# The inverses of a chunked recurrence: 32x32 blocks on four tiles of TensorE's array instead of 64x64 blocks on two

## The reference

```python
def rwkv7_scan(r, logw, k, v, kk, a, s0):
    def step(s, inp):
        r_t, lw_t, k_t, v_t, kk_t, a_t = inp
        sa = jnp.einsum('bhvk,bhk->bhv', s, -kk_t)
        s = (s * jnp.exp(lw_t)[:, :, None, :] + sa[..., None] * (kk_t * a_t)[:, :, None, :]
             + v_t[..., None] * k_t[:, :, None, :])
        return s, jnp.einsum('bhvk,bhk->bhv', s, r_t)
```

## Time and profile before

| | |
|---|---|
| median of 3 executions | 1626.25 us (1624.93 to 1627.86) |
| span of the profiled execution, first to last instruction | 1624.6 us |
| span plus what lies around it, at the median | 1626.25 us, so 1.65 us around |
| TensorE busy | 1540.8 us, 95% of the span |
| VectorE busy | 557.3 us, 34% |
| ScalarE busy | 298.2 us, 18% |

### The profile page before, as it was taken

One profiled execution on the slowest core, in us unless ns is written; L12 is line 12 of the kernel. 1 busy time (PEld: TensorE's weight loads), 2 busy tenths in 40 slices (PEclk: granted clock), 3 DMA queues, 4 the chain that ended last, 5 costly groups with the idle time before them and its releaser, 6 DMA issues.

```text
span 1624.6 us, 61645 instructions
## 1 busy us (share of the span) xinstructions
PE 1540.8 (95%) x27605; PEld 1373.6 (85%) x27605; DVE 557.3 (34%) x1410; ACT 298.2 (18%) x801; POOL 16.4 (1%) x32
## 2 busy tenths in 40 slices
PE   5999898999997999999988899999999999999995
PEld 3888476999546788988877898999999999999995
DVE  1463425666635354565771321010100101010102
ACT  2012422100111512434323201010101001010101
POOL 0000000000000000000000000000000000000000
PEclk9999999999999999999999899999999999999998
DMA  9722666444456233000123399999999999999993
GB/s 392 270 94 96 263 256 260 178 186 157 181 195 259 78 105 144 5 7 5 33 98 115 124 413 381 390 412 387 418 381 417 384 418 377 418 378 418 367 419 142
DMA packets 72892, 407.02 MB, mean 251 GB/s; under 512 B 10514, under 2 KB 10948, under 8 KB 35908
## 3 DMA queue, kind: packets, MB, share of 16 engines
q1 hardware_dynamic: 68176, 398.92, 62.0%
q0 software_dynamic: 1184, 3.41, 0.7%
q10 hardware_dynamic: 3412, 2.93, 0.5%
HBM read 403.31 MB, written 1.92 MB: 249 GB/s over the span
## 4 chain that ended last, share of the span: by engine, by line
PE 81%; PEld 10%; DVE 3%; ACT 2%; issue 2%; DMA 1%; ACTq 0%; PEldq 0%; DVEq 0%; POOL 0%
PE bank L1416 20%; PE bank L1436 10%; PE bank L953 8%; PEld bank L1416 6%; PE bank L986 4%; PE bank L625 4%; PE bank L628 4%; PEld bank L1436 3%; PE bank L730 3%; PE bank L733 3%; PE bank L1165 2%; PE bank L1125 2%; PE bank L651 2%; PE bank L755 2%; PE bank L1161 2%; PE bank L1150 2%
## 5 line engine op out<-in xcount | busy, mean ns | idle before, releaser
L1416 PE MATMUL bank<-w,ring 128*64 128x86 f32 x11264 | 455.0, 237 | 3.4 <-issue 2.8
L1416 PEld LDWEIGHTS bank<-w,ring 128*64 128x64 f32 x11264 | 434.4, 136 | 12.6 <-issue 11.6
L1436 PE MATMUL bank<-w,ring 128*64 128x86 f32 x5632 | 240.4, 238 | 0.9 <-issue 0.9
L2790 DVE TENSOR_TENSOR w<-w,bank 128x86 f32<-128x86 f32 x176 | 43.1, 245 | 554.4 <-PE bank L1416 545.8
L1436 PEld LDWEIGHTS bank<-w,ring 128*64 128x64 f32 x5632 | 222.4, 137 | 1.1 <-issue 1.1
L1921 ACT ACTIVATE w<-bank 128x86 f32<-128x86 f32 x176 | 42.8, 243 | 576.7 <-PE bank L1416 576.7
L625 PE MATMUL bank<-w,ring 128*128 128x256 f32 x256 | 57.6, 387 | 5.9 <-DVE w L2404 5.4
L625 PEld LDWEIGHTS bank<-w,ring 128*128 128x128 f32 x256 | 49.4, 194 | 14.2 <-DVE w L2404 5.6
L628 PE MATMUL bank<-ring,w 128*128 128x256 f32 x256 | 57.5, 387 | 1.9 <-DVE w L1986 1.9
L628 PEld LDWEIGHTS bank<-ring,w 128*128 128x128 f32 x256 | 49.6, 195 | 9.1 <-DVE w L1986 2.1
L1165 PE MATMUL bank<-ht 64*64 64x64 f32 x1280 | 49.7, 219 | 0.0
(11 more groups left out here) (432 smaller groups left out, 1890.1 us busy)
## 6 DMA issues: line engine op xcount, KB each, us to landing
ring<-in_moe_gu SPq DMA_DIRECT2D x176, 1024.0 KB, 8.4
ring<-in_moe_w_down SPq DMA_DIRECT2D x176, 512.0 KB, 8.6
ring<-in_ada_w SPq DMA_DIRECT2D x48, 1024.0 KB, 5.1
ring<-in_ev_w_in SPq DMA_DIRECT2D x11, 1024.0 KB, 25.7
ring<-in_ffn_w_gate SPq DMA_DIRECT2D x11, 1024.0 KB, 6.6
ring<-in_ffn_w_up SPq DMA_DIRECT2D x11, 1024.0 KB, 4.9
ring<-in_ffn_w_down SPq DMA_DIRECT2D x11, 1024.0 KB, 6.4
ring<-in_ev_w_out SPq DMA_DIRECT2D x4, 1024.0 KB, 10.9
```

The source lines that it names most:

```text
L1416: ins = [mm(b[hp, 0:CAP], w[:, k, hp], XG[:, k, :], start=k == 0, stop=k == KC - 1, skip_group_check=True) for hp in HALVES]
L1436: ins = [mm(bank[4 + c // 4][hp, (c % 4) * CAP:(c % 4 + 1) * CAP], w[:, c * P + hp.start:c * P + hp.stop], HIDU[:, t % 2, :], start=t == 0 ...
L2790: v.tensor_tensor(HIDU[:, t % 2, :], SILU[:, t % 2, :], bank[2 + t % 2][:, 0:CAP], ALU.mult).then_inc(sem("hid"), 1)
```

## The change: what it does

In levels 1 to 4, `z` and `xp` no longer multiply the 64x64 blocks. They multiply only the two 32x32 blocks on the diagonal of each: the array is addressed as four tiles of 32 rows by 32 columns on its diagonal (`QUARTERS`: partitions 0 to 31, 32 to 63, 64 to 95, 96 to 127). Each such product streams 32 columns through 32 columns of weights. Where there was one product of 64x64 there are two of 32x32. Level 5 and all other work stay as they were. ScalarE's and VectorE's instructions are the same as before and copy the same shapes; entries outside the 32x32 blocks are stale in the banks, and the masks of levels 1 to 4 never pick them. The semaphores still rise by two for each direction, now with the products of the third and the fourth tile.

```diff
+        QUARTERS = [(slice(32 * b, 32 * b + 32), slice(32 * (b % 2), 32 * (b % 2) + 32)) for b in range(4)]
+        ALL = slice(0, DH)
+        def cols(j, c):
+            return slice(j * DH + c.start, j * DH + c.stop)
...
                     for j in range(4):
-                        for hp in HALVES:
-                            ins = mm(bank[d][hp, j * DH:(j + 1) * DH], M4[i % 2][d][hp, j, 0, hp], IX[hp, d, j, :],
-                                     start=True, stop=True)
-                            if j == 3:
-                                ins.then_inc(sem(f"z{d}"), 1)
+                        if lv < 5:
+                            for b, c in QUARTERS:
+                                ins = mm(bank[d][b, cols(j, c)], M4[i % 2][d][b, j, 0, b], IX[b, d, j, c],
+                                         start=True, stop=True)
+                                if j == 3 and b.start >= 64:
+                                    ins.then_inc(sem(f"z{d}"), 1)
...
             def xp(i, lv):
                 for d in range(2):
                     pe.wait_ge(sem("zc"), 10 * i + 2 * (lv - 1) + d + 1)
                     if lv < 5:
                         for j in range(4):
+                            for b, c in QUARTERS:
+                                mm(bank[2 + d][b, cols(j, c)], IP[i % 2][b, d, j, c], IZ[b, d, j, c],
+                                   start=True, stop=True)
+                        for j in range(4):
+                            for b, c in QUARTERS:
+                                ins = mm(bank[2 + d][b, cols(4 + j, c)], IZ[b, d, j, c], IP[i % 2][b, d, j, c],
+                                         start=True, stop=True)
+                                if j == 3 and b.start >= 64:
+                                    ins.then_inc(sem(f"xp{d}"), 1)
+                    else:
+                        for j in range(4):
                             for hp in HALVES:
...
```

More of the change, by code:

```diff
@@ L1148, in z @@
                     for j in range(4):
-                        for hp in HALVES:
-                            ins = mm(bank[d][hp, j * DH:(j + 1) * DH], M4[i % 2][d][hp, j, 0, hp], IX[hp, d, j, :],
-                                     start=True, stop=True)
-                            if j == 3:
-                                ins.then_inc(sem(f"z{d}"), 1)
+                        if lv < 5:
[5 more added lines that the diff above has]
+                        else:
+                            for hp in HALVES:
+                                ins = mm(bank[d][hp, cols(j, ALL)], M4[i % 2][d][hp, j, 0, hp], IX[hp, d, j, :],
+                                         start=True, stop=True)
+                                if j == 3:
+                                    ins.then_inc(sem(f"z{d}"), 1)
             def xp(i, lv):
@@ L1159, in xp @@
                         for j in range(4):
-                            for hp in HALVES:
[L1161 to L1168, removed]
+                            for b, c in QUARTERS:
[4 more added lines that the diff above has]
+                                ins = mm(bank[2 + d][b, cols(4 + j, c)], IZ[b, d, j, c], IP[i % 2][b, d, j, c],
+                                         start=True, stop=True)
+                                if j == 3 and b.start >= 64:
+                                    ins.then_inc(sem(f"xp{d}"), 1)
+                    else:
+                        for j in range(4):
+                            for hp in HALVES:
+                                ins = mm(bank[2 + d][hp, cols(4 + j, ALL)], IZ[hp, d, j, :], IP[i % 2][hp, d, j, :],
+                                         start=True, stop=True)
+                                if j == 3:
+                                    ins.then_inc(sem(f"xp{d}"), 1)
             def right_side(i):
```

## The result

The changed kernel takes **1679.78 us** (median of 4 executions, 1678.36 to 1680.72). The kernel before, run beside it, takes 1626.01 us (4 executions, 1624.93 to 1627.86). The ratio is 1.033, with a 95% interval of 1.032 to 1.035. The forecast was 1609 us with a range up to 1638: wrong in sign and far out of range.

What follows compares the result with a forecast made beforehand. TensorE's stream of matmul passes was taken to bound the recurrence. A middle pair summed to -5.1 + 0.85 + 0.37 + 1.0 + 0.3 = -2.6 us, all pairs -18.9, with missed waits -17.4: from 1626.25 to 1609 us, range 1602 to 1638.

Steps and rivals of the forecast that it cites:

- So I take 32 / 4 = 8 ns a pass (7.9 unrounded).: z and xp, levels 1 to 4: 768 passes at 7.9 ns, 0.254 us a group, saving 5.1 us a middle pair.
- Changes of shape, +0.14 each: Where 64x64 steps meet z and xp of levels 1 and 2: six new changes, +0.85 us a pair.
- carry no longer overlaps: Carry, between two changes of shape, loses its cover by xp and costs its full 0.47: +0.37 us a pair.
- Waits for masked, 1.4 us a pair: TensorE waits for VectorE's masking before t4: 0.3, 0.8 and 0.3, together 1.4 in place of 0.4, +1.0 us.
- this loop: t4 (1.13 us), masking (1.29 us) and hops between them, claimed to be what is late next in a pair.
- The clock: I cost it at nothing too.: Recurrence: TensorE idles some 1.5 us in 24.4, in spread pieces under 1 us; the granted clock was expected to cost nothing.
- the first rival: Recurrence passes limited to 14.5 ns by issue: +1.5 us a pair, 1637 us; slower by the pass's price had chance 0.28.
- a row showed passes 14.5 ns apart: Overlap of carry with xp's tail: four passes per 58 ns on four tiles, for a tenth of a us.
- the far bound: At 29 ns a pass, the 384 added passes cost 11.1 us a pair; all ends some 90 us later, called improbable.
- 25 ns between starts of matmuls: If held across tiles, 768 passes take an estimated 19 us a pair; the trace showed starts 0.01 us apart.

Runs made afterwards that it cites:

- experiments 2 and 7: 2: changed kernel without levels 1-4 products for two of four systems, 1606.37 us; 7: kernel before with 32x32 z in levels 3, 4, pairs 1-6 only, 1622.98 us.
- experiment 1: The changed kernel with the same 32x32 products in z and xp, each streaming 64 columns instead of 32: 1671.46 us, ratio 1.029.
- experiment 9: The kernel before with 1024 unread small float32 products, then 1024 in bfloat16, written out behind TensorE's last product: 1699.15 us.
- experiment 10: The kernel before with 3072 unread small float32 products behind TensorE's last one, in loops of 64, 128 and 256 products: 1683.94 us.
- experiment 3: The kernel before with the 32x32 products in level 3 alone, levels 1, 2 and 4 in 64x64: 1631.94 us, ratio 1.005.

## Why the prediction was wrong, step by step

- *"So I take 32 / 4 = 8 ns a pass (7.9 unrounded)."* Nearly right, for as long as instructions last: groups of 32 passes in 0.27 and 0.28 us in place of 0.254, 8.4 to 8.8 ns a pass. Over the 24 groups of a pair that is 0.5 us or so too little.
- *Changes of shape, +0.14 each.* Right at full clock: solve and carry take 0.61 us (`727.21 0.61 PE bank L1233 x16`), and carry no longer overlaps.
- *Waits for masked, 1.4 us a pair.* The place was right, and the size nearly: TensorE is idle for 1.1 us before t4 in the pair from 695.30 us (`L1132 PE MATMUL bank<-ring 64*128 64x256 f32 x32 | 4.5, 399 | 1.1 <-DVE ring L2518 1.0`), 0.4 before the change. Stalls stand in the same pair, so it isn't a clean measure; without stalls (experiments 2 and 7) this loop is indeed what is late next.
- *"The clock: I cost it at nothing too."* Wrong, by about 8 us as far as experiment 1 can tell. In the rows it fell where stalls and small products with 32 columns came together.
- **The step that failed** is the rejection of the first rival, "the passes can't come closer than 14.5 ns in the long run (issue, not the array, limits them)". Its mechanism was the true one, and its price was too low by half: 3.5 to 4.0 us for 128 passes is 27 to 31 ns. I set it aside because a row showed passes 14.5 ns apart and the columns explained that figure. But that row is 0.1 us long, and a short burst is served from what has been brought already. The sentence on the far bound, that 29 ns was "improbable, as four tiles were denser than that", rests on the same burst. The rows had the number: over long stretches nothing was denser than 29 ns, and I read that as the array's price for 64 columns. It is that too: 8 groups of 0.466 us make 3.73 us for 64 products, about as much as their instructions take to arrive. The two limits lie on top of each other in this kernel, and so the second could not be seen behind the first. The far bound, about 90 us, was the nearest of my numbers in kind: the array's gain hides under the supply, and the t4 give some slack, so it became 54.

The Trainium skill, in "Runtime: NRT & Kernel Launch", section "Instruction fetch mechanics", says that each engine's instructions stream in by blocks of 16 KiB through a queue that the sequencer drives, and that the cost at a block's end is mostly hidden. The block size agrees (24 packets of 16,384 bytes for 6,144 instructions). The cost is hidden in the recurrence of the kernel before, which has no stall of over 0.25 us, and not in the dense code here: in experiment 9 TensorE stood still for 1.5 to 2.8 us of every 3.7. The same section of the Trainium skill says that kernels prefer to be unrolled, as a taken branch can force a fetch; in experiment 10 the loops took 18 to 22 ns where the unrolled code took 57. The prediction had also weighed the rule of the Trainium skill in "TensorE: Matmul & The Clock Gate", section "Wait — 56ns, not 53.3ns?", of 25 ns between starts of matmuls. Across tiles the runs go against it: 32 passes in 0.27 us are 8.4 ns apart.

## What to carry to other kernels

Before you split a product into smaller ones, count the instructions: for straight-line code on this engine, take 64 neighbouring float32 products (256 instructions), add up what the array needs for them, and if it is under some 3.7 us, expect the rest to be a stall, whatever the average over a longer stretch says. It is a warning and no exact count: the kernel before has 128 passes within 3.4 us in each of its middle pairs and no stall, perhaps since they lie across a packet's end, and beside large loads a stretch took up to 5.9 us in the changed kernel. Split only beside long instructions (t4 here), or inside a loop whose body is held. And when an engine stands still in the middle of equal instructions with no releaser, measure from stall to stall and count: a constant number of instructions means supply.

## What the runs showed of the hardware that was not expected

- TensorE's instructions arrive 256 at a time, where they are awaited every 3.5 to 4.0 us, of which the transfer itself is 0.9 to 1.5 (experiment 9); 24 more packets in the queue "instruction" for 6,144 more instructions. Loops of 64, 128 and 256 products (16 to 64 KB) need 7 packets in all, and no long stall comes after their first round.
- While other loads held the DMA engines at 0.99 of their time (experiment 3, 797.13 to 799.93 us), no packet of instructions started.
- Four 32x32 tiles in turn take 8.4 to 8.8 ns a pass at full clock (0.27 and 0.28 us for 32 passes), and 9.0 ns in the loop of 256 (4.60 us for 512).
- In two kernels with the same products and stalls at the same rhythm, the clock of the six middle pairs was 0.84 to 0.90 with 32 columns a product (the changed kernel) and 1.00, once 0.95, with 64 (experiment 1). The stalls were shorter in the second (up to 1.6 against 2.2 us in these pairs), so columns and idle time are not told apart. In the written-out stretch behind the kernel's end the clock was 0.50 from 1615 us on, in the rounds of the loops without stalls 1.00.

What stays open: what a recurrence with its pairs in a loop would take. Its buffers turn by twos and threes, so with a period of six pairs, and one pair's code is 138 KB long (540 products of 256 bytes), above the 64 KB of the longest body tried, so this is a rewrite, and it wasn't tried. Open is also why the clock fell, and whether moving the large loads away from the recurrence would take the longest stalls out.
